# Choice of experts in finer steps, the first expert tile's rows from the ranks, half the context units later

## The chip, the cores and the metric

The kernel runs on one core of one Trainium2 chip. The metric is device time in microseconds. Each engine (PE for matmuls, DVE, ACT, POOL, and SP, which only issues transfers) runs its own instruction list; they meet at semaphores alone.

## The reference, cut to what matters

Two layers run in sequence, all in fp32, on 512 tokens of width 1024. The first ends in a hierarchical mixture of experts, 4 groups of 8 experts; the second begins with a projection of which the part called "context" here (a matmul of 256 context tokens, then a 5-tap convolution and a SiLU) needs nothing of the first layer.

```python
def hierarchical_moe(h, w_group, b_group, w_expert, b_expert, w_gate_up, w_down):
    g_logits = (t @ w_group + b_group).astype(jnp.float32)
    g_onehot = jax.nn.one_hot(jnp.argmax(g_logits, -1), N_GROUPS, dtype=jnp.float32)
    e_logits = (jnp.einsum('td,gde->tge', t, w_expert) + b_expert).astype(jnp.float32)
    e_sel = jnp.einsum('tge,tg->te', e_logits, g_onehot)
    top_vals, top_idx = lax.top_k(e_sel, TOP_K)      # 2 of the group's 8
    ...
    for g in range(N_GROUPS):
        gu = jnp.einsum('td,edf->tef', t, w_gate_up[g]).astype(jnp.float32)
        act = jax.nn.silu(a) * b * gate[:, g, :, None]
        y = y + jnp.einsum('tef,efd->td', act, w_down[g].astype(jnp.float32))
```

## The kernel before

**Up to the choice.** `out1_pe` ends the first mixer's output projection for four tiles of 128 tokens, transposes each normalised tile (`turn(t)`, `p.turns`, L154) and multiplies it with the router's 36 columns (`logits(t)`, L142). `route_dve` then chooses for all four tiles at once: the group by its largest logit, the best two of its experts by compares with rank numbers (`first_of`), and the sum AS of the two one-hot masks (signal `chosen`). `Chain` makes every step wait for the one before it on DVE.

**Ranks and indices.** `route_pe` counts with triangular and all-one matmuls how many earlier tokens want the same expert (`ranks`, L1192, L1194). `route_dve` makes from it prefix sums over the 32 experts (a copy and five shifted adds), where each token's row goes, and the mask S (`selected`); eight 128x32 matmuls (`row_ids`, L142) give the list of tokens of every expert tile (`token_ids`), and later `expert_ids`.

**Expert tiles.** There are eight groups g of four experts. Tile 2g ("home") holds 32 tokens for each; tile 2g+1 ("spill") holds overflow tokens of any expert. Here `up(j, third)` is 16 matmuls of 128x512 for one half of gate and up, `hidden(j)` two transposes, `down(j)` 16 matmuls. `experts_pool` fetches the tokens of tile j from memory (a gather, L1430); `rows(j)` on PE transposes them in eight matmuls (L154) into banks 0 and 1, and `rows(j)` on ACT and on DVE copy one bank each.

**Weights.** 96 pieces of 1 MB (twelve for each group: two times four for gate and up, four for down) go through SP's queue: the first 18 in the order `FIRST`, with the four context weights (`ctx_weights`, 1 MB each in rows of 1 KB) put in by `CTX_BEFORE`, and those in `AFTER_ROWS` held until `rows(0)` is done. `experts_sp` then issues pieces 18 to 95, each when the piece that held its buffer (15 in `SLOTS`, three used once in `ONCE`) is used up. ACT issues a spill tile's pieces conditionally (`spill`), by numbers that `spill_ids` loads into registers.

**Context.** `ctx_conv(p, a, b)` issues units a to b of 64. A unit is one matmul of 128x256 (two passes, two trace records). Eight units make a block b, in bank 2 or 7 in turn; `ctx_take(b)` on ACT empties the bank (`ctx_taken`), DVE makes the taps, `ctx_silu(b)` on ACT ends it. All 64 units stand between the logits and the first `up`, where PE otherwise waits. `keep_busy` is dummy work of five matmuls.

```python
        ctx_conv(p, 21, 46)
        p.wait_ge(S("selected"), 1)
        p.acc(bk(1, 32), sel, inc=S("row_ids"))
        ctx_conv(p, 46, 61)
```

Of the kernel before, what the change touches and what calls it, by code (L numbers as in the profile page):

```python
# [231 lines left out]
def program(nc, A, out):  # L232
# [973 lines left out]

    def route_dve(v):
        gl = lg[:, :, 0:4]
        el = lg[:, :, 4:36].rearrange("p t (g e) -> p t g e", g=4)
# [5 lines left out]
        c.red(gm[:, 0:4], gl, ALU.max)
        c.tt(v4(oh), gl, b4(gm[:, 0:4], 4), ALU.is_equal)
        c.tt(v4(ky), v4(oh), C["rank4"].unsqueeze(1).to_broadcast([P, 4, 4]), ALU.mult)
        c.red(km[:, 0:4], v4(ky), ALU.max)
        c.tt(v4(oh), v4(ky), b4(km[:, 0:4], 4), ALU.is_equal)
        es, e1, o1, o2, kk8, e2 = (rt0[:, 96 + 32 * j:128 + 32 * j] for j in range(6))  # L1220
        big = rt0[:, 320:448]
        bv = big.rearrange("p (t g e) -> p t g e", t=4, g=4)
        ohb = v4(oh).unsqueeze(3).to_broadcast([P, 4, 4, 8])
        c.tt(bv, el, ohb, ALU.mult)
        c.red(v8(es), big.rearrange("p (t g e) -> p t e g", t=4, g=4), ALU.add)
        m1, m2 = gm[:, 4:8], gm[:, 8:12]

        def first_of(dst, src, m):
            c.tt(v8(dst), v8(src), b4(m, 8), ALU.is_equal)
            c.tt(v8(kk8), v8(dst), C["rank8"].unsqueeze(1).to_broadcast([P, 4, 8]), ALU.mult)  # L1230
            c.red(km[:, 4:8], v8(kk8), ALU.max)
            c.tt(v8(dst), v8(kk8), b4(km[:, 4:8], 8), ALU.is_equal)

        c.red(m1, v8(es), ALU.max)
        first_of(o1, es, m1)
        c.stt(e2, o1, -3e38, es, ALU.mult, ALU.add)
        c.red(m2, v8(e2), ALU.max)
        first_of(o2, e2, m2)
        v.wait_ge(S("logit_m"), 4)
        v.up(v.e.memset(AS5[:, 128:160], 0.0), None)  # L1240
        c.tt(v4d(A1), ohb, v8(o1).unsqueeze(2).to_broadcast([P, 4, 4, 8]), ALU.mult)
        c.tt(v4d(A2), ohb, v8(o2).unsqueeze(2).to_broadcast([P, 4, 4, 8]), ALU.mult)
        c.tt(AS, A1, A2, ALU.add, inc=S("chosen"))


        pad = [MIX[:, 416 + 96 * j:512 + 96 * j].rearrange("p (s n) -> p s n", s=2) for j in range(2)]
# [2747 lines left out]
```

## Time and profile before

| | |
|---|---|
| runs of the kernel | 2337.04 us (median of 3), 2333.0 to 2340.38 |
| profiled execution: its own time (span, first to last instruction) | 2333.6 us |
| PE busy in it | 2212.6 us, 95% |
| DVE, ACT, POOL busy | 56%, 33%, 10% |
| memory read and written, mean over the span | 182 GB/s |

The span is the only time that the page gives for the profiled execution; no part of it outside the span is listed. PE is busy nearly always, but a share of the whole span says little of one stage: the page's DMA row in 40 slices reads 8 or 9 of ten from slice 4 to slice 10 (175 to 583 us), while PE's row reads 8 in slices 7 and 8 (350 to 467 us). Stages are therefore read one by one.

### The profile page before, as it was taken

How to read it: one execution, taken by the hardware profiler on the slowest of the kernel's cores; microseconds unless marked ns; L12 is line 12 of the kernel's file. 1: busy time of each engine (PE TensorE's matmuls, PEld its weight loads, DVE VectorE, ACT ScalarE, POOL GpSimd, SP SyncE). 2: the span in 40 equal slices, each digit the busy share in tenths (PEclk: the TensorE clock that was granted, in tenths of full speed). 3: DMA queues.
4: the chain of work that ended last, by engine and by line, in shares of the span. 5: the costliest groups of instructions: out<-in, count | busy, mean ns of one | idle time of the engine just before them, and what ended most of it. 6: DMA issues, size and time to landing. Idle time of an engine off the chain costs nothing.

```text
span 2333.6 us, 31012 instructions
## 1 busy us (share of the span) xinstructions
PE 2212.6 (95%) x12750; PEld 1721.4 (74%) x12750; DVE 1301.8 (56%) x2050; ACT 774.9 (33%) x1324; POOL 233.7 (10%) x219
## 2 busy tenths in 40 slices
PE   8999998899999999999999999999889889999997
PEld 6765843335889896788888888867777667788886
DVE  3355622215766786767686764436666645444444
ACT  3346111113534553512111120235556544222222
POOL 0000011101050440000000000002021040000000
PEclk9999999999999999999999999999999999999999
DMA  7548889998203114233343331111010203322321
GB/s 253 175 143 289 310 320 416 417 415 300 71 23 109 64 46 155 102 105 127 108 145 126 109 109 54 55 52 46 1 59 19 73 1 102 100 97 90 108 91 54
DMA packets 141084, 317.28 MB, mean 136 GB/s; under 512 B 16534, under 2 KB 77310, under 8 KB 128400
## 3 DMA queue, kind: packets, MB, share of 16 engines
q1 hardware_dynamic: 123136, 259.55, 31.1%
q0 software_dynamic: 16928, 52.55, 6.4%
q10 hardware_dynamic: 880, 3.20, 0.4%
q8 instruction: 101, 1.65, 0.3%
q14 instruction: 39, 0.32, 0.0%
HBM read 408.54 MB, written 15.79 MB: 182 GB/s over the span
## 4 chain that ended last, share of the span: by engine, by line
PE 79%; DVE 10%; DMA 5%; ACT 5%; issue 1%; POOL 0%; DVEq 0%; SPq 0%; ACTq 0%
PE PS L142 35%; PE PS L2995 12%; PE PS L721 5%; PE PS L1746 4%; PE PS L1453 4%; PE PS L154 3%; PE PS L2923 2%; PE PS L3623 2%; PE PS L1004 2%; PE PS L1465 2%; PE PS L148 2%; PE PS L3544 2%; DVE X L112 1%; DVE Rr L112 1%; PE PS L1056 1%
## 5 line engine op out<-in xcount | busy, mean ns | idle before, releaser
L142 PE MATMUL PS<-at,wH 128*128 128x512 f32 (+1 forms) x2144 | 564.0, 352 | 1.8 <-DVE at L112 1.8
L142 PEld LDWEIGHTS PS<-at,wH 128*128 128x128 f32 x2144 | 378.1, 189 | 61.1 <-issue 5.3
L142 PE MATMUL PS<-at,rest 128*128 128x512 f32 (+1 forms) x1072 | 376.4, 351 | 0.0
L2995 PE MATMUL PS<-wH,ac 128*128 128x512 f32 x880 | 278.1, 393 | 3.3 <-DVE hn L112 3.3
L142 PEld LDWEIGHTS PS<-at,rest 128*128 128x128 f32 x1072 | 202.6, 189 | 27.3
L112 DVE TENSOR_TENSOR rest<-ring,wH 128x2048 fp32r<-128x2048 f32 x66 | 150.3, 2289 | 95.5 <-ACT wH L135 95.4
L2995 PEld LDWEIGHTS PS<-wH,ac 128*128 128x128 f32 x880 | 165.2, 188 | 43.8 <-DVE hn L112 8.4
L135 ACT CAST wH<-ring 128x2048 fp32r<-128x2048 f32 x66 | 124.6, 1906 | 201.0 <-PE PS L2995 201.0
L2995 PE MATMUL PS<-rest,ac 128*128 128x512 f32 x440 | 171.4, 390 | 0.0
L112 DVE TENSOR_TENSOR hn<-PS,gate 128x512 f32<-128x512 f32 x120 | 83.0, 692 | 86.0 <-PE PS L2995 79.3
L135 ACT CAST ac<-sil 128x1536 fp32r<-128x1536 f32 (+1 forms) x22 | 27.8, 1264 | 296.0 <-DVE sil L112 296.0
L112 DVE TENSOR_TENSOR sil<-sil,PS 128x512 f32<-128x512 f32 x66 | 39.1, 598 | 153.6 <-PE PS L142 153.6
L2995 PEld LDWEIGHTS PS<-rest,ac 128*128 128x128 f32 x440 | 82.7, 188 | 17.0 <-issue 0.7
L132 ACT ACTIVATE sil<-PS 128x512 f32<-128x512 f32 x66 | 34.7, 527 | 178.2 <-PE PS L142 178.2
L1453 PE MATMUL PS<-ring,AT 128*32 128x512 f32 x288 | 87.5, 600 | 4.8 <-DMA R<-in_w_gate_up_dram 3.0
L112 DVE TENSOR_TENSOR H<-H,hn 128x512 f32<-128x512 f32 x120 | 83.0, 692 | 4.1
L135 ACT COPY R<-PS 128x512 f32<-128x512 f32 (+4 forms) x105 | 47.4, 471 | 107.9 <-PE PS L142 58.6
L142 PE MATMUL PS<-Rr 96*128 96x512 f32 (+3 forms) x384 | 80.8, 345 | 1.3 <-ACT Rr L135 1.3
L123 DVE TENSOR_REDUCE sm<-PS 128x1 f32<-128x768 f32 x64 | 60.9, 952 | 36.7 <-PE PS L142 36.2
L1453 PE MATMUL PS<-R,AT 128*32 128x512 f32 x400 | 75.2, 616 | 5.5 <-DMA HIw<-in_w_gate_up_dram 2.4
L154 PE MATMUL PS<-con,R 128*128 128x128 f32 (+1 forms) x452 | 66.3, 278 | 14.3 <-DVE R L116 8.0
L154 PEld LDWEIGHTS PS<-con,R 128*128 128x128 f32 (+1 forms) x452 | 50.8, 140 | 37.0 <-DVE R L116 11.6
(503 smaller groups left out, 4503.4 us busy)
## 6 DMA issues: line engine op xcount, KB each, us to landing
R<-in_w_gate_up_dram SPq DMA_DIRECT2D x25, 1024.0 KB, 13.9
R<-in_w_gate_up_dram ACTq DMA_DIRECT2D x25, 1024.0 KB
HIw<-in_w_ada_dram POOLq DMA_DIRECT2D x24, 1024.0 KB, 5.6
ring<-in_w_ffn_gate_dram SPq DMA_DIRECT2D x22, 1024.0 KB, 5.4
ring<-in_w_ffn_up_dram SPq DMA_DIRECT2D x22, 1024.0 KB, 5.4
ring<-in_w_ffn_down_dram SPq DMA_DIRECT2D x22, 1024.0 KB, 4.9
ring<-in_w_gate_up_dram SPq DMA_DIRECT2D x18, 1024.0 KB, 11.8
ring<-in_w_gate_up_dram ACTq DMA_DIRECT2D x18, 1024.0 KB
```

The lines of the kernel that those rows point to most:

```text
L112: return self.up(self.e.tensor_tensor(dst, a, b, op), inc)
L123: return self.up(self.e.tensor_reduce(dst, a, AX, op, negate=neg), inc)
L135: return self.up(self.e.copy(dst, src), inc)
L142: ins = self.e.matmul(out, l, r, start=k == 0, stop=k == len(pairs) - 1)
L148: ins = self.e.matmul(o, l, r, start=True, stop=True)
L154: ins = self.e.transpose(o, i_, ident[0:i_.shape[0], 0:i_.shape[0]])
L721: ins = p.e.matmul(bk(t), x, w[:, k, :], start=r == 0 and k == 0 and i == 0, stop=r == 1 and k == 3 and i == 2)
L1004: ins = p.e.matmul(bk(g % 3), x, w, start=k == 0 and i == 0, stop=k == 7 and i == 2)
L1453: ins = p.e.matmul(PS[32 * c:32 * c + 32, 512 * b:512 * b + 512], hgT[j % 2][:, 4 * third + k, 32 * c:32 * c + 32], expert_slot(g, third, ...
L1465: ins = p.e.matmul(PS[32 * c:32 * c + 32, 512 * (5 + h):512 * (6 + h)], abT[j % 2][:, 128 * f + 32 * c:128 * f + 32 * c + 32], expert_slot ...
L1746: ins = p.e.matmul(bk(i % 4), x, y[:, k, :], start=b == 0 and k == 0 and n == 0, stop=b == 1 and k == 3 and n == 2)
L2995: ins = p.e.matmul(bk(4 + n_dn % 3), a_, b_, start=start and i == 0, stop=stop and i == len(terms) - 1)
```

## The change

The logits of a tile start when half of it is copied. The choice becomes `choose(v, t0, n)`, run for tiles 0 and 1, for tile 2 and for tile 3 apart, with DVE's max and max_index of eight; the rank matmuls of tiles 0 to 2 precede the last choice. A compare S0 (128x512) and four matmuls of one column give the tokens of tile 0 (`first_ids`), for which the first gather now waits in place of `token_ids`. Prefix sums become two scans. `rows(0)` goes to banks 5 and 6, both copied by ACT, and `row_ids` stands inside `up(0, 0)`. Six context units move behind `up(0, 1)`, 32 into groups 2 and 3; context weights 2 and 3 are loaded behind piece 26 into buffers that pieces 9 and 10 have left, and pieces 14 and 15 no longer wait for `rows(0)`. Blocks 4 to 7 of the context all use bank 7.

```diff
@@ out1_pe, route_pe @@
+            for k in range(8):
+                if k % 4 == 0:
+                    p.wait_ge(S("h1_T_copy"), 2 * t + k // 4 + 1)
...
         logits(2)
-        ctx_conv(p, 2, 6)
         turn(3)
-        ctx_conv(p, 6, 8)
+        ctx_conv(p, 2, 3)
         logits(3)
-        ctx_conv(p, 8, 21)
+        ctx_conv(p, 3, 5)
...
-    CTX_W = [(R[:, 4096:6144], ("o", 4)), (H[:, 4096:6144], ("gate_kept", 64)), (R[:, 8192:10240], ("normed_T", 4)), (R[:, 0:2048], ("out1", 8))]
-    ctx_bank = lambda b: (2, 7)[b % 2]
+    CTX_W = [(R[:, 4096:6144], ("o", 4)), (H[:, 4096:6144], ("gate_kept", 64)), (H[:, 0:2048], ("down", 4)), (H[:, 2048:4096], ("down", 4))]
+    ctx_bank = lambda b: 2 if b in (0, 2) else 7
...
-                p.wait_ge(S("ctx_taken"), b - 1)
+                p.wait_ge(S("ctx_taken"), b - 1 if b < 4 else b)
...
+        p.e.matmul(at(3, 5), ones, tile(2, 2), start=False, stop=False)
+        ctx_conv(p, 5, 7)
+        p.wait_ge(S("chosen"), 3)
+        p.e.matmul(at(3, 4), C["U"], tile(3, 1), start=False, stop=False)
+        ins = p.e.matmul(at(4, 5), ones, tile(3, 1), start=False, stop=True)
         p.up(ins, S("ranks"))
-        ctx_conv(p, 21, 46)
-        p.wait_ge(S("selected"), 1)
-        p.acc(bk(1, 32), sel, inc=S("row_ids"))
-        ctx_conv(p, 46, 61)
+        ctx_conv(p, 7, 9)
+        p.wait_ge(S("first_rows"), 1)
+        p.acc(bk(3, 1), [(S0[:, 128 * t:128 * t + 128], less[:, t:t + 1]) for t in range(4)], inc=S("first_row_m"))
+        ctx_conv(p, 9, 24)
@@ choose (tiles t0 to t0 + n), route_dve @@
+        c.red(gm[:, ts_], gl, ALU.max)
+        c.tt(of4(oh), gl, of(gm, 4), ALU.is_equal)
+        c.tt(of4(ky), of4(oh), C["rank4"].unsqueeze(1).to_broadcast([P, n, 4]), ALU.mult)
+        c.red(km[:, ts_], of4(ky), ALU.max)
+        c.tt(of4(oh), of4(ky), of(km, 4), ALU.is_equal)
+        c.ts(of4(pen), of4(oh), 1.0, 3e38, ALU.subtract, ALU.mult)
+        c.tt(bv, el, of4(pen).unsqueeze(3).to_broadcast([P, n, 4, 8]), ALU.add)
...
+            v.up(v.e.max(mx8[:, 8 * t:8 * t + 8], big[:, 32 * t:32 * t + 32]), None)
...
+            v.up(v.e.max_index(ix8[:, 8 * t:8 * t + 8].bitcast(U32), mx8[:, 8 * t:8 * t + 8], big[:, 32 * t:32 * t + 32]), None)
+        c.copy(ixf[:, 8 * t0:8 * t0 + 8 * n], ix8[:, 8 * t0:8 * t0 + 8 * n].bitcast(U32))
...
+        for A_, j in ((A1, 0), (A2, 1)):
+            v.tt(v32(A_)[:, ts_, :], iot[:, 0:32].unsqueeze(1).to_broadcast([P, n, 32]),
...
+        c.tt(S0.rearrange("p (t n) -> p t n", t=16), bc(m0, 32), iot[:, 1:33].unsqueeze(1).to_broadcast([P, 16, 32]), ALU.is_equal, inc=S("first_rows"))
...
-        for j, sh in enumerate((1, 2, 4, 8, 16)):
-            src, dst = pad[j % 2], pad[1 - j % 2]
-            c.tt(dst[:, :, 16:48], src[:, :, 16:48], src[:, :, 16 - sh:48 - sh], ALU.add)
+        for j, x in enumerate((spill, free)):
+            v.up(v.e.tensor_tensor_scan(tally[:, j, 1:33], ones[:, 0:32], x, 0.0, ALU.mult, ALU.add), None)
+        v.wait_ge(S("first_row_m"), 1)
+        v.ts(tidx0, bk(3, 1), 4096.0, None, ALU.add, inc=S("first_ids"))
@@ weights, gathers @@
-    FIRST = [5, 1, 3, 4, 12, 13, 0, 2, 7, 8, 16, 6, 17, 9, 10, 11, 14, 15]
-    CTX_BEFORE = {5: 0, 12: 1, 0: 2, 7: 3}
-    AFTER_ROWS = (11, 14, 15)
+    FIRST = [5, 1, 14, 3, 4, 12, 13, 0, 2, 15, 7, 8, 16, 6, 17, 9, 10, 11]
+    CTX_BEFORE = {5: 0, 12: 1}
+    AFTER_ROWS = (11,)
...
             expert_piece(s, m)
+            if m == 26:
+                for i in (2, 3):
+                    ctx_weights(s, i)
...
-        g.wait_ge(S("token_ids"), 1)
+        g.wait_ge(S("first_ids"), 1)
...
+            if j == 1:
+                g.wait_ge(S("token_ids"), 1)
@@ experts_pe, experts_act @@
+                if j == 0 and third == 0 and k == 2:
+                    p.wait_ge(S("selected"), 1)
+                    p.acc(bk(1, 32), sel, inc=S("row_ids"))
...
         rows(0)
-        ctx_conv(p, 61, 64)
+        ctx_conv(p, 24, 26)
...
             up(2 * g, 1)
+            if g == 0:
+                ctx_conv(p, 26, 32)
+                rows(1)
...
             down(2 * g)
+            if g in (2, 3):
+                ctx_conv(p, 16 * g, 16 * g + 8)
             if g not in (0, NG - 1):
                 up(2 * g + 1, 1)
             if g + 1 < NG:
                 rows(2 * g + 3)
+            if g in (2, 3):
+                ctx_conv(p, 16 * g + 8, 16 * g + 16)
...
                 rows(2 * g + 3)
                 ids = spill_ids(g + 1)
             if 1 <= g < 5:
+                if g in (2, 3):
+                    ctx_take(a, 2 * g)
+                    ctx_take(a, 2 * g + 1)
```

**PE from the last choice to the first expert tile.** In the rows, `L1056` (now `L1059`) is a context unit, `L154` (`L155`) the transposes of `rows(0)`, `L1453` (`L1486`) an `up`; `s_exp1` is `ctx_taken`. Before:

```order
L142 MATMUL PS<-X,MIX 128x32 [waits s_chosen]
L142 MATMUL PS<-X,MIX 128x32 x7
L1056 MATMUL PS<-AT,R 128x256 x2
L1056 MATMUL PS<-AT,R 128x256 [waits s_exp1,s_x_in3]
L1056 MATMUL PS<-AT,R 128x256 x7
L1056 MATMUL PS<-AT,R 128x256 [waits s_exp1]
L1056 MATMUL PS<-AT,R 128x256 x4
L154 MATMUL PS<-con,MIX 128x128 [waits s_rows0]
L154 MATMUL PS<-con,MIX 128x128 x7
L1056 MATMUL PS<-AT,R 128x256 x3
L1453 MATMUL PS<-ring,AT 32x512 [waits s_rowsD,s_w_home00,s_rowsA,s_exp1]
```

`row_ids` leads this stretch, and 15 units follow it up to `rows(0)`. Now, from the last rank matmul:

```order
L1205 MATMUL PS<-MIX,con 128x32
L1059 MATMUL PS<-AT,R 128x256 x2
L143 MATMUL PS<-MIX 128x1 [waits s_first_rows]
L143 MATMUL PS<-MIX 128x1 x3
L1059 MATMUL PS<-AT,R 128x256 x7
L1059 MATMUL PS<-AT,H 128x256 [waits s_exp1,s_ada_w1]
L1059 MATMUL PS<-AT,H 128x256 x7
L155 MATMUL PS<-con,MIX 128x128 [waits s_rows0]
L155 MATMUL PS<-con,MIX 128x128 x7
L1059 MATMUL PS<-AT,H 128x256 [waits s_exp1]
L1059 MATMUL PS<-AT,H 128x256
L1486 MATMUL PS<-ring,AT 32x512 [waits s_w_home00,s_rowsA]
```

The eight 128x32 matmuls have left the place ahead of `rows(0)`, four of one column have come, and 15 context units stand behind these, where 15 stood behind `row_ids` before and 25 ahead of it.

**PE at the end of group 2.** `L154` (`L155`) with the wait for `s_rows1` is `rows(7)`, `L690` (`L691`) is `keep_busy`, and `s_w_home01` is the next home tile's weights. Before:

```order
L1453 MATMUL PS<-R,AT 32x512 x3
L154 MATMUL PS<-con,MIX 128x128 [waits s_rowsD,s_rowsA,s_rows1]
L154 MATMUL PS<-con,MIX 128x128 x7
L690 MATMUL PS<-con 128x128 x5
L1453 MATMUL PS<-HIw,AT 32x512 [waits s_w_home01]
L1453 MATMUL PS<-HIw,AT 32x512
```

Nothing but dummies stands between the transposes and the next `up`. Now:

```order
L1486 MATMUL PS<-R,AT 32x512 x3
L155 MATMUL PS<-con,MIX 128x128 [waits s_rowsD,s_rowsA,s_rows1]
L155 MATMUL PS<-con,MIX 128x128 x7
L1059 MATMUL PS<-AT,H 128x256 [waits s_exp1]
L1059 MATMUL PS<-AT,H 128x256 x7
L691 MATMUL PS<-con 128x128 x5
L1486 MATMUL PS<-HIw,AT 32x512 [waits s_w_home01]
L1486 MATMUL PS<-HIw,AT 32x512
```

A block of eight units with a wait for `ctx_taken` stands between `rows(7)` and the next home tile; another block (not shown) stands ahead of the spill tile's second half.

**ACT at the end of group 2.** `TENSOR_LOAD sm` rows are the register loads of `spill_ids(3)`, `s_masked` stands for DVE's taps. Before:

```order
L1529 TENSOR_LOAD sm
L1529 ISA x2
L1530 TENSOR_LOAD sm
L1530 ISA x2
L132 ACTIVATE AT<-MIX,cwc 128x256 [waits s_masked] x2
L1536 ISA [waits s_up]
L1536 DMA HIw<-in_w_gate_up_dram 128x2048
```

ACT goes from the loads straight to the SiLUs of the context. Now, with `s_o` for `ctx_conv`:

```order
L1568 TENSOR_LOAD sm
L1568 ISA x2
L1569 TENSOR_LOAD sm
L1569 ISA x2
L136 COPY AT<-PS 128x256 [waits s_o] x2
L133 ACTIVATE AT<-MIX,cwc 128x256 [waits s_masked] x2
L1575 ISA [waits s_up]
L1575 DMA HIw<-in_w_gate_up_dram 128x2048
```

The two copies that empty bank 7 stand behind the eight register loads, and behind the copy of `rows(7)` ahead of those.

## Rows read from the trace of the kernel before

**Rows 1.** Table by stage: stretch, us; PE, PEld, DVE, ACT, POOL busy; PEclk, DMA share, GB/s.

```profile
246.00:250.00 4.00, 4.00 (x19) 3.25 (x19) 3.72 (x7) 0.20 (x1) 0.00 (x0) 1.00 1.09 390
282.00:286.00 4.00, 4.00 (x24) 3.64 (x24) 3.01 (x18) 0.37 (x1) 0.00 (x0) 1.00 1.02 426
294.00:316.00 22.00, 22.00 (x163) 13.01 (x163) 6.16 (x19) 5.87 (x11) 5.10 (x5) 1.00 0.60 218
370.00:530.00 160.00, 138.44 (x1170) 58.96 (x1166) 36.27 (x70) 20.23 (x37) 17.10 (x17) 0.97 1.01 416
429.00:433.00 4.00, 3.91 (x24) 0.98 (x28) 0.00 (x0) 0.00 (x0) 0.00 (x0) 0.57 1.01 416
```

**Rows 2.** PE's timeline around the choice and the first expert tiles.

```profile
274.05 1.98 PE L142 MATMUL PS<-X,MIX 128*128 128x36 f32 x16
...
293.64 1.87 PE L142 MATMUL PS<-X,MIX 128*128 128x32 f32 x16
295.35 6.72 PE L1056 MATMUL PS<-AT,R 128*128 128x256 f32 x30
301.90 1.05 PE L154 MATMUL PS<-con,MIX 128*128 128x128 f32 x8
...
304.18 0.62 PE L1453 MATMUL PS<-ring,AT 128*32 128x512 f32 x1
...
312.30 0.59 PE L1453 MATMUL PS<-ring,AT 128*32 128x512 f32 x1
```

**Rows 3.** DVE's timeline, same stretch: last normalised tile, choice, ranks, indices.

```profile
268.95 1.28 DVE L120 SCALAR_TENSOR_TENSOR H<-H,X 128x1024 f32<-128x1024 f32 x1
...
270.69 0.20 DVE L112 TENSOR_TENSOR X<-PS,X 128x36 f32<-128x36 f32 x1 [0.34 <-PE PS L142]
276.07 0.20 DVE L112 TENSOR_TENSOR X<-PS,X 128x36 f32<-128x36 f32 x1 [5.18 <-PE PS L142]
...
281.23 0.29 DVE L112 TENSOR_TENSOR MIX<-MIX 128x128 f32<-128x128 f32 x1
...
282.96 0.19 DVE L117 TENSOR_SCALAR MIX<-PS 128x32 f32<-128x32 f32 x1 [0.54 <-PE PS L1194]
...
291.61 1.22 DVE L112 TENSOR_TENSOR MIX<-con,MIX 128x1024 f32<-128x1024 f32 x1
...
295.55 0.19 DVE L116 TENSOR_SCALAR sm<-PS 128x32 uint32<-128x32 f32 x1 [0.93 <-PE PS L142]
```

**Rows 4.** POOL's timeline: the first gather's issue.

```profile
296.63 1.09 POOL L1430 DMA_INDIRECT MIX<-h1d,sm  x1 [17.58 <-DVE sm L116]
```

**Rows 5.** The gathers' line (L1430) over the kernel: issue to landing.

```profile
DMA to landing us min/median/max: 4.5/8.3/12.7
```

**Rows 6.** The h1d write of L1167, issued at 270.5 under the weight stream: landing.

```profile
DMA to landing us min/median/max: 9.5/9.5/9.5
```

**Rows 7.** ACT's timeline at the end of group 2.

```profile
381.22 0.59 ACT L135 COPY AT<-PS 128x512 f32<-128x512 f32 x1 [0.23 <-PE PS L154]
386.06 0.51 ACT L132 ACTIVATE AT<-MIX,cwc 128x256 f32<-128x256 f32 x1 [4.25 <-issue]
```

**Rows 8.** What PE waited for between 380 and 410.

```profile
PE PS L1453 <- DMA ring<-in_w_gate_up_dram: 2.7, 1, 2.7
PE PS L1453 <- DMA X<-in_w_gate_up_dram: 0.9, 1, 0.9
PE PS L1465 <- DMA R<-in_w_down_dram: 0.7, 1, 0.7
```

**Rows 9.** Three expert pieces (L1405) issued at 316 into idle queues: landing.

```profile
DMA to landing us min/median/max: 5.3/6.4/7.5
```

**Rows 10.** The chain that ended last: one expert piece in the full stream.

```profile
391.95 14.01 DMA R<-in_w_down_dram
```

**Rows 11.** PE's timeline in group 4: the first matmul behind a gap.

```profile
429.09 1.06 PE L1453 MATMUL PS<-HIw,AT 128*32 128x512 f32 x1 [2.41 <-DMA gate<-in_w_gate_up_dram]
```

More of the change, by code:

```diff
@@ L988, in logits @@
             p.wait_ge(S("conv_w"), 1)
-            p.acc(bk(3 + t % 2, 36), [(hT[:, k, 128 * t:128 * t + 128], wr[:, k, :]) for k in range(8)], inc=S("logit_m"))
+            for k in range(8):
+                if k % 4 == 0:
+                    p.wait_ge(S("h1_T_copy"), 2 * t + k // 4 + 1)
+                ins = p.e.matmul(bk(3 + t % 2, 36), hT[:, k, 128 * t:128 * t + 128], wr[:, k, :], start=k == 0, stop=k == 7)
+            p.up(ins, S("logit_m"))
         def ctx_turn(t):
@@ L1188, in route_pe @@
     def route_pe(p):
-        p.wait_ge(S("chosen"), 1)
-        tile = lambda q, n: v32(AS)[:, q, :].unsqueeze(1).to_broadcast([P, n, 32])
+        tile = lambda q, n: AS_of(q).unsqueeze(1).to_broadcast([P, n, 32])
+        at = lambda a_, b_: bk(0, 160).rearrange("p (t n) -> p t n", t=5)[:, a_:b_, :]
+        p.wait_ge(S("chosen"), 2)
         p.e.matmul(bk(0, 160), C["U"], AS5, start=True, stop=False)
-        for q in range(4):
-            ins = p.e.matmul(bk(0, 160).rearrange("p (t n) -> p t n", t=5)[:, q + 1:5, :], ones, tile(q, 4 - q),
-                             start=False, stop=q == 3)
+        p.e.matmul(at(1, 5), ones, tile(0, 4), start=False, stop=False)
@@ L1196, in route_pe @@
+        p.e.matmul(at(2, 5), ones, tile(1, 3), start=False, stop=False)
+        p.e.matmul(at(3, 5), ones, tile(2, 2), start=False, stop=False)
[3 more added lines that the diff above has]
+        ins = p.e.matmul(at(4, 5), ones, tile(3, 1), start=False, stop=True)
         p.up(ins, S("ranks"))
-        ctx_conv(p, 21, 46)
-        p.wait_ge(S("selected"), 1)
-        p.acc(bk(1, 32), sel, inc=S("row_ids"))
@@ L1200, in route_pe @@
-        ctx_conv(p, 46, 61)
+        ctx_conv(p, 7, 9)
+        p.wait_ge(S("first_rows"), 1)
+        p.acc(bk(3, 1), [(S0[:, 128 * t:128 * t + 128], less[:, t:t + 1]) for t in range(4)], inc=S("first_row_m"))
+        ctx_conv(p, 9, 24)
     def route_act(a):
+        for b in range(3):
+            ctx_take(a, b)
+        for h in range(2):
+            a.wait_ge(S("rows_T"), h + 1)
+            a.cast(hgT[0][:, 4 * h:4 * h + 4, :], bk(5 + h).rearrange("p (k t) -> p k t", k=4), inc=S("rowsA"))
@@ L1214, in route_dve @@
         c = Chain(v)
[L1215 to L1246, printed above, removed]
@@ L1249, in route_dve @@
         small = [MIX[:, 800 + 8 * j:808 + 8 * j] for j in range(12)]
-        less = MIX[:, 1984:2000]
-        for x in pad:
-            v.up(v.e.memset(x[:, :, 0:16], 0.0), None)
-        for j in range(4):
-            c.ts(less[:, 4 * j:4 * j + 4], C["tid"], 4096.0 - (S_ if j == 3 else 0.0), None, ALU.subtract)
+        v.wait_ge(S("ranks"), 1)
+        r4, m4 = bk(0, 128).rearrange("p (t n) -> p t n", t=4), m0.rearrange("p (t n) -> p t n", t=4)
+        v.settle()
+        v.tt(m4[:, 0:3, :], r4[:, 0:3, 0:4], v32(AS)[:, 0:3, 0:4], ALU.mult)
+        v.tt(m4[:, 3, :], r4[:, 3, 0:4], AS3[:, 0:4], ALU.mult)
+        c.tt(S0.rearrange("p (t n) -> p t n", t=16), bc(m0, 32), iot[:, 1:33].unsqueeze(1).to_broadcast([P, 16, 32]), ALU.is_equal, inc=S("first_rows"))
         magic = 12582912.0
-        spill, free = pad[0][:, 0, 16:48], pad[0][:, 1, 16:48]
-        v.wait_ge(S("ranks"), 1)
-        c.ts(spill, bk(0, 32, 128), 48.5, 1.0 / 32, ALU.subtract, ALU.mult)
+        spill, free = wants[:, 0:32], wants[:, 32:64]
+        v.ts(spill, bk(0, 32, 128), 48.5, 1.0 / 32, ALU.subtract, ALU.mult)
         v.ts(free, bk(0, 32, 128), 32.5, None, ALU.is_lt)
@@ L1264, in route_dve @@
         c.ts(spill, spill, magic, 0.0, ALU.subtract, ALU.max)
[L1265 to L1269 removed]
+        v.settle()
+        for j, x in enumerate((spill, free)):
+            v.up(v.e.tensor_tensor_scan(tally[:, j, 1:33], ones[:, 0:32], x, 0.0, ALU.mult, ALU.add), None)
+        incl, before, taken = tally[:, 0, 1:33], tally[:, 0, 0:32], tally[:, 1, 1:33]
+        v.wait_ge(S("first_row_m"), 1)
+        v.ts(tidx0, bk(3, 1), 4096.0, None, ALU.add, inc=S("first_ids"))
         c.stt(RV, before, 64.0, C["hh"], ALU.mult, ALU.add)
[L1273 removed]
+        v.tt(freecode, free, taken, ALU.mult)
         c.ts(RV, RV, 512.0, -1.0, ALU.mult, ALU.add)
@@ L1518, in silu @@
             a.wait_ge(S("hidden"), j - 1)
-            a.fn(sil[j % 2], bk(2 + j % 2, 256), ACT.Silu, inc=S("silu"))
+            a.fn(sil[j % 2], bk(hid_bank(j), 256), ACT.Silu, inc=S("silu"))
         def y(j):
@@ L1542, in experts_act @@
         a.fn(sm[:, 64:65], ones[:, 0:1], ACT.Silu)
-        rows(0)
-        ctx_take(a, 7)
         ids = spill_ids(0)
+        spill(0, 0)
         rows(1)
+        ctx_take(a, 3)
         for g in range(NG):
-            spill(g, 0)
+            if g:
+                spill(g, 0)
             if g:
@@ L1607, in ctx_taps @@
                 c.stt(to, src, cwc[:, b, tap:tap + 1], to, ALU.mult, ALU.add, inc=S("ctx_sum") if tap == 4 else None)
-        rows(0)
         rows(1)
```

84 lines of the change are left out of this document (55 added, 29 removed).

## The prediction

> **What bounds the kernel now.** I read first the table by stage, to see whether transfers or PE fill each stretch. From 370 to 530 the DMA share is 1.01 at 416 GB/s and PE is busy for 138.44 of 160 us: the experts' weights set the pace there, and PE waits. From 294 to 316 it is the reverse: PE is busy for all 22.00 us, with a DMA share of 0.60 [rows 1], so transfers stand idle for 0.40 x 22 = 8.8 us. The stream of pieces 18 to 95 starts when the first home tile is used up, so the whole stage moves with the start of the first spill tile, 312.30 [rows 2]; but no earlier start can give more than those 8.8 us. Second I read the timelines of PE, DVE and POOL for the chain that leads there: last logits read by DVE at 276.07, last mask 281.23, ranks 282.96, token list 295.55 [rows 3], gather issued 296.63 [rows 4], rows transposed 301.90, first `up` 304.18 [rows 2]. PE has no gap in it: the context units are what it does while DVE chooses.
>
> **The chain up to the first expert tile.** *Logits.* The last tile is normalised at 268.95 + 1.28 = 270.2 [rows 3]. Its logits ran from 274.05 to 276.03, behind six context units; one is left. A unit is 6.72 / 15 = 0.45 us [rows 2], so five give 2.2: logits end at 273.8. *Choice.* It took from 276.07 to 281.23 + 0.29 = 281.52, in steps of about 0.2 [rows 3]. The pass for tile 2, some 15 steps from 270.69 + 0.20, ends at about 274.2, just behind those logits; that for tile 3 has 13 steps, 2.6 us, behind one read of 0.2, so it ends at 277.1, 4.4 earlier. max and max_index don't occur in the trace; I count them as the other small steps, 0.2; at 0.5 each it is 1 us more, at nothing 1 us less. *Ranks.* 281.52 to 282.96 was 1.4 for five matmul groups; two are left behind the last mask: 0.7, so 277.8. *First rows.* Two small steps and a 128x512 compare, for which I take 0.7, between 0.29 for 128 and 1.22 for 1024 columns [rows 3]: 278.9. Four matmuls and one step are half of the eight and their step (293.64 [rows 2] to 295.74 [rows 3], 2.1) with a little for the hand-over: 280.2. From token list to gather it was 0.9 [rows 3, 4], so the gather is issued at 281.1, 15.5 earlier. The scans are beside this path.
>
> *Landing.* This is the term without a row of its own. Before, the gather met idle transfers; at 281 the share is 1.02 [rows 1]. Gathers took 4.5 to 12.7, median 8.3 [rows 5], and a write issued from the same queue at 270.5 in this very stretch took 9.5 [rows 6]. I take 9.0, nearest to that write: 290.1. The ends are 4.5 and 12.7. The Trainium skill, "DMA: Bandwidth & Descriptors", section "Issuing engines are not separate DMA queues", says that transfers of all issuing engines share the same 16 DMA engines and interleave, which speaks against an early gather under another queue's stream; the 9.5 against 4.5 agrees. If it did not hold, the sum would come out by 3.6 us lower.
>
> *PE.* Behind the ranks stand 17 units and four small matmuls, 7.7 + 0.9, so PE is free at 286.5 and idle for 3.6. Transposes to first `up` took 304.18 - 301.90 = 2.3 [rows 2]; with one unit less on the path I take 2.0: 292.1, or 12.1 earlier.
>
> **What is given back at once.** From first `up` to the spill tile it was 312.30 - 304.18 = 8.1 [rows 2]. `row_ids` comes into it (1.87, of which 1.7 between its neighbours [rows 2]), six units (2.7), and about 0.8 because the second gather now waits for a token list made inside this stretch and ACT loads registers ahead of the second tile's copy: 13.3 and 305.4. The stream's start moves by s = -6.9. With a landing of 4.5 PE itself is the limit at 286.5, so s = -10.5; with 12.7, s = -3.2. As 6.9 is less than 8.8, the transfers' idle time can take it. Pieces 14 and 15 cost nothing: the same 18 pieces are through before the stream starts, in idle time if need be.
>
> **The full stream.** Context weights 2 and 3 lay ahead of it and now lie in it. A piece of 1 MB is 1.05 / 0.416 = 2.5 us [rows 1]. These come in rows of 1 KB: from 246 to 250, where such rows flow among others, 390 GB/s need a share of 1.09, against 426 at 1.02, or 1.17 times the time for a byte [rows 1]; if half the bytes there were context weights, 1.34. I take 3.1 each, so +6.2 (bounds 5.0 and 6.7). Of s, -0.7 is left.
>
> **PE in groups 2 and 3.** Sixteen units a group are 16 x 0.45 = 7.2. The second block stalls besides: bank 7 is emptied by ACT behind the copy at 381.22 and the register loads, during which ACT does nothing until 386.06, 4.25 us of it without a releaser [rows 7]. So PE waits about 386.06 - 381.22 = 4.8 each time, and is 2 x (7.2 + 4.8) = 24.0 later. Three waits for weights in these groups vanish: 2.7 + 0.9 + 0.7 = 4.3 [rows 8]. PE then falls behind its weights by 24.0 - 4.3 - 6.2 = 13.5. How much of that the transfers bear is the depth of the queue: a piece in the full stream lands 14.0 after its issue [rows 10], one in an idle queue after 5.3 [rows 9], so 8.7 us of work lie queued. The remaining 13.5 - 8.7 = 4.8 is idle time of a resource that is busy to the end of the stage, and is not got back: +4.8. The waits behind it (21.6 us without PE work from 370 to 530 [rows 1], the 4.3 among them) let PE catch up, no more.
>
> **The clock.** A gap of 2.41 us ahead of 429.09 was followed by matmuls of 1.06 us [rows 11] where full speed has 0.59 [rows 2]; the granted clock was 0.57 from 429 to 433 [rows 1], the lower level (1.2 GHz) for most of it. Four steps at twice their time, some 3.4 us, cost half of that, 1.7. The two stalls are longer than that gap. From 370 to 530 its mean is 0.97 beside those 21.6 us of gaps [rows 1], so it follows not every gap, and I take one of two: +1.7.
>
> **Sum.** -6.9 + 6.2 + 4.8 + 1.7 = +5.8. The profiled execution's span of 2333.6 would become 2339.4; it is 3.4 below the median of the runs, 2337.0, and to that I add: **2342.8 us**. 0.3%, or 7.0 us, is about what a measurement of this kernel can tell from no change.
>
> **Rivals.** *Clock and late gather (slower).* The clock falls in both stalls (+1.7), and also in the idle 3.6 ahead of the first tile (+1.7): 2346.2; if the gather lands after 12.7 as well, 3.7 more, 2349.9. This is slower than can be missed as soon as any 1.2 us come on top of the forecast. The gaps are longer than that of rows 11; against it, one clock loss early may fall into the 1.9 us of idle transfers that s leaves. The Trainium skill, "TensorE: Matmul & The Clock Gate", section "Why this matters for your kernels", warns that idle gaps between bursts of matmuls send the array back to the lower clock; rows 11 agree, and by it this rival would be the forecast. *Transfers alone.* If PE's lag stays within the depth, because the queue bears more than 8.7 or more of the idle 21.6 comes early, only s and the weights count: -0.7, 2336.3, and with s = -10.5 it is 2332.7. For it: share 1.01; against it: 24 us of work in two groups that had 4.3 of waits. *All kept (faster).* If the context weights slip in for nothing and PE's work fits its waits, s alone remains: 2330.1, and 2328.2 where the gather lands early and s takes all of the 8.8. Rows 1 with a share of 1.01 speak against it. *No earlier tile.* If another queue entry holds the gather up until the stream thins out, near 294, s is about -3.2 and the time 3.7 over the forecast, 2346.5; its chance is counted with the first rival, whose late gather it is.
>
> **Chances.** Forecast 0.40 (0.07 of it above 7.0 more than before), clock or late gather 0.28, transfers alone 0.20 (0.01 of it below -7.0), all kept 0.12 (0.09 below). So faster 0.10, same 0.55, slower 0.35. The range runs from 2331, just under the transfers' rival with the early landing, to 2352: s = -3.2, both clock losses and the upper price of the weights give 2337.0 - 3.2 + 6.7 + 4.8 + 3.4 + 1.7 = 2350.4, and a stall a little longer makes the rest. About 0.1 lies below and 0.1 above.
>
> **What would show it.** Steps right: last mask near 277, gather 0 issued near 281 and landed near 290, first `up` near 292, spill tile near 305; in groups 2 and 3 PE waits of some 5 us for ACT's copy of bank 7, and a stretch between 385 and 440 where the DMA share is below 1. Wrong: a share of 1.01 throughout (transfers alone), a gather that lands within 5 us, PE waits for `ctx_taken` below 2 us, or PEclk of 1.00 behind both stalls.

## The result and the profile after

The changed kernel takes 2348.45 us (median of 6 runs, 2347.18 to 2351.48), the kernel before 2335.28 (6 runs, 2332.67 to 2340.96): a ratio of 1.0051, interval 1.0039 to 1.0063, or 12 us slower. The profiled execution has a span of 2346.5, the one of before 2333.6: +12.9. From the page of the changed kernel, the span and PE's total:

```profile
span 2346.5 us, 31053 instructions
...
PE 2216.0 (94%) x12760; PEld 1722.3 (73%) x12760; DVE 1304.1 (56%) x2072; ACT 774.8 (33%) x1325; POOL 233.9 (10%) x219
```

PE's busy time has hardly changed (2212.6 us before). The table by stage (columns as in rows 1) tells where the time went:

```profile
370.00:530.00 160.00, 143.17 (x1146) 69.41 (x1139) 34.72 (x68) 19.65 (x39) 16.15 (x16) 0.97 0.92 373
390.00:400.00 10.00, 9.27 (x54) 6.39 (x58) 1.89 (x4) 1.55 (x4) 0.00 (x0) 0.83 0.98 406
400.00:410.00 10.00, 9.48 (x84) 3.51 (x80) 1.12 (x2) 0.59 (x1) 1.00 (x1) 1.00 0.42 153
430.00:440.00 10.00, 7.64 (x26) 6.34 (x26) 3.55 (x8) 1.23 (x4) 0.00 (x0) 0.66 0.99 414
440.00:450.00 10.00, 9.48 (x82) 3.56 (x85) 1.12 (x2) 0.90 (x2) 0.10 (x1) 1.00 0.15 34
```

From 370 to 530 the DMA share is 0.92 where it was 1.01 [rows 1]. The missing share lies in two holes: 0.42 from 400 to 410 and 0.15 from 440 to 450, that is (1.01 - 0.42) x 10 + (1.01 - 0.15) x 10 = 14.5 us of idle transfers. Ahead of each, PE ran at a granted clock of 0.83 and 0.66.

**The head came out as worked out, up to the gather.** The second tile's logits, in the trace of before and then in that of the changed kernel, where the timeline goes on to the first spill tile:

```profile
265.17 1.87 PE L142 MATMUL PS<-X,MIX 128*128 128x36 f32 x16
```

```profile
266.07 1.87 PE L992 MATMUL PS<-X,MIX 128*128 128x36 f32 x16
...
290.69 1.16 PE L155 MATMUL PS<-con,MIX 128*128 128x128 f32 x8 [3.02 <-DMA MIX<-h1d,sm]
...
293.48 1.06 PE L1486 MATMUL PS<-ring,AT 128*32 128x512 f32 x1
...
295.18 0.59 PE L1486 MATMUL PS<-ring,AT 128*32 128x512 f32 x1
...
296.14 1.97 PE L143 MATMUL PS<-X,MIX 128*128 128x32 f32 x16
...
306.02 1.04 PE L155 MATMUL PS<-con,MIX 128*128 128x128 f32 x8
308.42 0.62 PE L1486 MATMUL PS<-ring,AT 128*32 128x512 f32 x1 [1.36 <-ACT AT L136]
```

This execution ran 0.9 late there, as it did at the first tile's logits (257.96 against 257.06), ahead of all that was changed; so I count from the second tile's. The first `up` comes at 293.48 - 266.07 = 27.4 (before 39.0), the first spill tile at 42.35 (before 47.1 [rows 2]): 4.8 earlier, 3.9 on the span's own scale. Of 11.6 us at the first `up` more than half is gone fifteen microseconds later. On DVE's timeline, one slow step of the last choice, the last mask, and the 128x512 compare:

```profile
275.87 0.91 DVE L118 TENSOR_SCALAR X<-X 128x4 f32<-128x4 f32 x1
...
278.10 0.19 DVE L113 TENSOR_TENSOR MIX<-MIX 128x32 f32<-128x32 f32 x1
...
279.29 0.69 DVE L113 TENSOR_TENSOR MIX<-X,con 128x512 f32<-128x512 f32 x1
```

The gather in the chain that ended last:

```profile
282.17 8.47 DMA MIX<-h1d,sm
```

**The stall.** ACT's timeline and PE's at the end of groups 2 and 3:

```profile
385.73 0.59 ACT L136 COPY AT<-PS 128x512 f32<-128x512 f32 x1 [0.23 <-PE PS L155]
390.31 0.37 ACT L136 COPY AT<-PS 128x256 f32<-128x256 f32 x1 [3.99 <-issue]
```

```profile
377.76 3.72 PE L1059 MATMUL PS<-AT,H 128*128 128x256 f32 x16
...
390.73 5.39 PE L1059 MATMUL PS<-AT,H 128*128 128x256 f32 x16 [4.59 <-ACT AT L136]
...
419.66 3.72 PE L1059 MATMUL PS<-AT,H 128*128 128x256 f32 x16
...
432.36 6.75 PE L1059 MATMUL PS<-AT,H 128*128 128x256 f32 x16 [4.32 <-ACT AT L136]
```

The copy of the rows at 385.73, then the register loads, then at 390.31 the copy that frees bank 7; PE's second block waits 4.59 and 4.32 for it, and takes 5.39 and 6.75 us where the first blocks take 3.72. Between them PE waits for nothing else of note from 380 to 440:

```profile
PE PS L1059 <- ACT AT L136: 8.9, 2, 4.6
```

No wait for weights is left there. The kernel before has 8.5 us of them in the same stretch: the 4.3 of rows 8, which end at 410, and from 410 to 440

```profile
PE PS L1453 <- DMA gate<-in_w_gate_up_dram: 2.4, 1, 2.4
PE PS L1453 <- DMA HIw<-in_w_gate_up_dram: 1.8, 1, 1.8
```

On SP's timeline one sees the other end. The row at 385.48 is of four pieces, issued within 20.30 us where the same four took 11.31 before: the last of them had to wait for its buffer. The next hole ends with the piece at 448.44, which went at 425.43 before. Before, then now:

```profile
380.97 11.31 SPq L1405 DMA_DIRECT2D R<-in_w_down_dram  x4
...
425.43 0.33 SPq L1405 DMA_DIRECT2D R<-in_w_down_dram  x1
```

```profile
385.48 20.30 SPq L1426 DMA_DIRECT2D R<-in_w_down_dram  x4
...
448.44 0.33 SPq L1426 DMA_DIRECT2D R<-in_w_down_dram  x1
```

The first matmul behind the experts, before and now:

```profile
553.17 0.50 PE L1746 MATMUL PS<-Xr,Hr 128*128 128x512 f32 x1
```

```profile
566.47 0.50 PE L1788 MATMUL PS<-Xr,Hr 128*128 128x512 f32 x1
```

It starts 300.40 us after the second tile's logits, 288.00 before: +12.4, in this execution the whole of the loss.

### The profile page after: what moved, and what is told of

The parts are those of the page before. It is cut to its first block, busy times and chain, and to the rows that moved or that the text cites. A ratio compares the mean times of both kernels' runs of the same rounds, so it can differ in the third digit from the quotient of the medians.

```text
span 2346.5 us, 31053 instructions
## 1 busy us (share of the span) xinstructions
PE 2216.0 (94%) x12760; PEld 1722.3 (73%) x12760; DVE 1304.1 (56%) x2072; ACT 774.8 (33%) x1325; POOL 233.9 (10%) x219
## 4 chain that ended last, share of the span: by engine, by line
PE 77%; DVE 11%; ACT 5%; DMA 4%; issue 1%; ACTq 0%; POOL 0%; DVEq 0%; SPq 0%; POOLq 0%
PE PS L143 34%; PE PS L3038 12%; PE PS L722 5%; PE PS L1486 4%; PE PS L155 3%; PE PS L1788 3%; PE PS L2966 2%; PE PS L1498 2%; PE PS L3666 2%; PE PS L1008 2%; DMA R<-in_w_gate_up_dram 2%; DVE X L113 2%; PE PS L3587 2%; PE PS L149 1%; DVE Rr L113 1%
## 5 line engine op out<-in xcount | busy, mean ns | idle before, releaser
L113 DVE TENSOR_TENSOR sil<-sil,PS 128x512 f32<-128x512 f32 x66 | 39.1, 598 | 153.7 <-PE PS L143 153.7
L1486 PE MATMUL PS<-ring,AT 128*32 128x512 f32 x288 | 88.6, 604 | 7.3 <-DMA R<-in_w_gate_up_dram 5.9
L155 PE MATMUL PS<-con,R 128*128 128x128 f32 (+1 forms) x452 | 66.6, 278 | 14.9 <-DVE R L117 8.1
L155 PEld LDWEIGHTS PS<-con,R 128*128 128x128 f32 (+1 forms) x452 | 50.8, 139 | 38.1 <-DVE R L117 11.7
L143 PEld LDWEIGHTS PS<-Rr 96*128 96x128 f32 (+1 forms) x384 | 64.7, 188 | 16.5 <-issue 3.5
```

Source lines behind the costliest of these rows:

```text
L113: return self.up(self.e.tensor_tensor(dst, a, b, op), inc)
L143: ins = self.e.matmul(out, l, r, start=k == 0, stop=k == len(pairs) - 1)
L155: ins = self.e.transpose(o, i_, ident[0:i_.shape[0], 0:i_.shape[0]])
L1486: ins = p.e.matmul(PS[32 * c:32 * c + 32, 512 * b:512 * b + 512], hgT[j % 2][:, 4 * third + k, 32 * c:32 * c + 32], expert_slot(g, third, ...
```

## The experiments

All ratios are to the kernel before. "Spill" and "end" are taken from PE's timeline of each profiled execution, counted from the second tile's logits: to the first spill tile's first matmul, and to the first matmul behind the experts. Each value is of one execution. The eight with the changed kernel's head (all but the kernel before, choice alone, move alone and the two with a new head) have spill tiles from 40.5 to 43.6, and the changed kernel's own two executions lie 1.7 apart there and 3.8 at the end. A difference of that size in these columns shows nothing by itself.

| run | ratio (interval) | spill | end |
|---|---|---|---|
| kernel before | 1 | 47.1 | 288.0 |
| changed kernel | 1.0051 (1.0039 to 1.0063) | 42.4 | 300.4 |
| the same, in a later job | 1.0051 (1.0038 to 1.0064) | 40.7 | 296.6 |
| bank 7 emptied first | 1.0001 (0.9987 to 1.0015) | 41.8 | 287.3 |
| the same, late units left out | 1.0003 (0.9990 to 1.0017) | 41.9 | 284.7 |
| the same, late weights left out | 0.9985 (0.9973 to 0.9997) | 43.6 | 285.3 |
| dummies in the stalls | 1.0061 (1.0040 to 1.0082) | 40.5 | 293.6 |
| dummies, in the later job | 1.0035 (1.0022 to 1.0048) | 40.7 | 294.4 |
| choice alone | 1.0038 (1.0020 to 1.0056) | 53.8 | 295.2 |
| move alone | 1.0049 (1.0031 to 1.0067) | 49.9 | 295.1 |
| late blocks spread | 0.9997 (0.9986 to 1.0008) | 40.5 | 283.1 |
| spread, new head | 0.9989 (0.9975 to 1.0003) | 39.1 | 284.2 |
| spread, new head, wide rows | 0.9988 (0.9979 to 0.9996) | 39.3 | 283.8 |

**Bank 7 emptied first.**

```diff
             y(2 * g)
             spill(g, 2)
+            if g in (2, 3):
+                ctx_take(a, 2 * g)
             if g not in (0, NG - 1):
...
                 if g in (2, 3):
-                    ctx_take(a, 2 * g)
                     ctx_take(a, 2 * g + 1)
```

> ACT empties bank 7 of the first late block right behind the spill issue of group 2 (and 3), ahead of the SiLU, the copy of the rows and the register loads; nothing else changes. Theory (the stalls for bank 7 and the half clock behind them cost the time): PE's waits of 4.6 and 4.3 us go, the second blocks take 3.65 us in place of 5.4 and 6.75, PE's lag at the end of group 3 falls from about 23 to about 10 us, DMA idle in 400 to 450 falls from 14.4 us to about 3 us, and the time to about 2336 (2334 to 2339). Rival (32 more units in a stage that transfers bound cost their own time, stall or not): 14.4 us of units remain as lag, transfers still idle, time 2342 to 2346.

Measured 2337.13, within the theory's bounds: the place of one copy is worth some 12 us. PE's two second blocks and the stage:

```profile
383.66 3.62 PE L1059 MATMUL PS<-AT,H 128*128 128x256 f32 x16
...
419.04 3.62 PE L1059 MATMUL PS<-AT,H 128*128 128x256 f32 x16
```

```profile
370.00:530.00 160.00, 148.81 (x1240) 69.84 (x1242) 36.16 (x70) 21.48 (x41) 17.10 (x17) 1.00 1.00 407
```

No block waits, all four take 3.6 to 3.7 us, the clock is 1.00 and the share 1.00.

**Dummies in the stalls.** `keep_busy(p, 2, 20)` ahead of the second blocks.

> Twenty dummy matmuls of 128x128 (about 4.5 us) stand ahead of the second late block in groups 2 and 3, where PE waits for bank 7: the stall keeps its length, but PE is busy in it. Theory: the granted clock stays at full speed, the blocks take 3.65 us, and 1.7 + 3.1 = 4.8 us of lag go, so the time falls by about 4 to 5 us, to 2344. Rival (the lower clock cost nothing, since PE waits behind it anyway): unchanged, 2348 (2347 to 2350).

The granted clock behind the two stalls did what was expected:

```profile
389.00:393.00 4.00, 3.85 (x20) 3.29 (x19) 1.45 (x3) 0.25 (x1) 0.00 (x0) 1.00 1.02 417
429.00:433.00 4.00, 4.00 (x22) 3.56 (x22) 1.70 (x4) 0.20 (x1) 0.00 (x0) 1.00 1.01 422
```

The time didn't show it: 2348.1, with an interval of 0.4%. So it was run again, beside the changed kernel.

> The kernel with dummies in the two stalls once more, in five rounds, beside the changed kernel itself: its four runs before lay at 2345 twice and at 2351 twice, and told nothing. Theory (half clock behind the stalls costs some 5 us of lag): 4 to 6 us below the changed kernel. Rival (lag that is spared there is given back behind the experts): within 2 us of the changed kernel.

> The changed kernel as it is, for comparison in the same job: 2347 to 2350 in either theory.

Now 2345.19 against 2350.75 (a little above the 2347 to 2350 expected), ratios 1.0035 and 1.0051. The intervals of the four runs overlap; some 3 to 4 us for the clock is likely, less than the 4.9 us by which the two blocks were long (5.39 + 6.75 - 2 x 3.6), and in time it is not settled. In the stage it is seen. The first execution with dummies:

```profile
370.00:530.00 160.00, 148.87 (x1237) 74.94 (x1236) 34.84 (x69) 20.08 (x39) 16.13 (x16) 1.00 0.95 386
```

The share is 0.95 in both executions with dummies and 0.92 in both of the changed kernel: 0.03 x 160 = 4.8 us less of idle transfers with the clock kept, and some 10 us still idle for the stall and the units. That the stall is the larger part shows in time too: with the clock kept, 8 us of loss remain in the better of the two jobs.

**Late units left out.** In `ctx_conv`, on top of the run that empties bank 7 first.

```diff
+            if b >= 4 and 0 < k < 7:
+                continue
```

> As the run that empties bank 7 first, and of each of the four late blocks only the first and the last matmul are kept, so that 24 of the 32 late units are left out (their part of the context is not computed). Theory (without the stall the remaining 14.4 us of units fit into PE's waits and the queue's depth): at most 3 us faster than that run, about 2334. Rival (the units themselves cost): faster than that run by 6 to 11 us.

2337.9: in this execution the experts end 2.6 earlier, and the time is no shorter. Three quarters of the units, 24 x 0.45 = 10.8 us of PE's work, cost next to nothing once the stall is gone. The stage, and the longest of the waits for weights that come back from 380 to 450:

```profile
370.00:530.00 160.00, 142.73 (x1198) 61.60 (x1194) 36.27 (x70) 21.51 (x41) 17.14 (x17) 0.98 1.01 414
```

```profile
PE PS L1488 <- DMA gate<-in_w_gate_up_dram: 2.2, 1, 2.2
```

**Late weights left out.** The two loads behind piece 26 are taken out of that same run, with the waits for them.

> As the run that empties bank 7 first, but context weights 2 and 3 are not loaded (their units read what the buffers hold, so that part of the context is not what it should be). Theory (the two loads of 1 MB in rows of 1 KB cost 6 us of a stage that transfers bound): the pieces behind piece 26 land 6 us earlier, the last expert tile ends 4 to 6 us earlier than in that run, time about 2332. Rival (PE, with 32 units more, is the limit there, and the loads are hidden): within 1.5 us of that run.

2332.93 against 2337.13, ratios 0.9985 and 1.0001: about 4 us, the theory's sign and two thirds of its size. The two intervals overlap, so the time alone does not show it. The landings do: the piece behind piece 26 landed 4.7 us after it, 9.2 in the run that empties bank 7 first, so it came 4.6 earlier, where 6 were expected. The experts' end came 2.1 earlier, not 4 to 6, behind a spill tile that was 1.8 later in this execution. The loads are not free, but the stream had some room for them. Their price is most of the 5 us by which the spill tile comes earlier, which may be why the run that empties bank 7 first is no faster than the kernel before.

**Choice alone.** `CTX_W`, banks, `FIRST`, `AFTER_ROWS` and `SLOTS` as before; the rest of the change stays.

```diff
-        ctx_conv(p, 9, 24)
+        ctx_conv(p, 9, 61)
...
         rows(0)
-        ctx_conv(p, 24, 26)
+        ctx_conv(p, 61, 64)
```

> The new choice, ranks, scans and first gather, but all 64 context units ahead of the first expert tile, and the context weights, their banks and pieces 14 and 15 as in the kernel before. Theory (ahead of the first tile PE is the limit, so that a shorter choice alone brings nothing): PE busy without a gap, first up at 303 to 304, first spill tile at 313 to 315, time 0 to 3 us above the kernel before, about 2337. Rival (the choice's chain was the limit): first up 4 to 12 us earlier than 304.2, time 2325 to 2331.

2343.26, slower than either theory said. The first part held: first `up` at 304.53, as before, behind PE's own work. What neither had is behind it:

```profile
304.53 0.62 PE L1483 MATMUL PS<-ring,AT 128*32 128x512 f32 x1
...
306.39 1.97 PE L143 MATMUL PS<-X,MIX 128*128 128x32 f32 x16
...
314.45 1.16 PE L155 MATMUL PS<-con,MIX 128*128 128x128 f32 x8 [0.80 <-DMA MIX<-h1d,sm]
318.67 0.62 PE L1483 MATMUL PS<-ring,AT 128*32 128x512 f32 x1 [3.06 <-ACT AT L136]
```

`row_ids` now stands inside the first `up`, so the second gather's list comes late (0.80 of wait at 314.45), and ACT's copy of those rows, behind its register loads, later still (3.06). The first spill tile starts 6.7 us later than before.

**Move alone.** The old choice with the late blocks, weights and piece order, bank 7 emptied first.

> The old choice, ranks and first gather, with the context units, the context weights, the order of the pieces and the emptying of bank 7 as in the run that empties it first; 32 units stay ahead of the first up, three of them behind rows(0). Theory (the choice is on the path only once the units are moved): PE idles some 10 us ahead of rows(0), first up at 303 to 304, first spill tile 0 to 1 us earlier than before, so 46 to 47 from the second tile's logits in place of 41.9, and the time 3 to 5 us above the run with both, about 2341. Rival (the choice brings nothing in any order): time equal to that run's, 2337.

2346.96: the sign is right, the size over twice what was expected, and the spill tile comes at 49.9 instead of 46 to 47. PE waits for the masks, the selection and the gather, with nothing to fill in, and in the stage from 294 the granted clock is 0.72:

```profile
281.53 0.54 PE L1192 MATMUL PS<-MIX,con 128*128 128x160 f32 x2 [2.87 <-DVE MIX L112]
...
293.93 3.62 PE L142 MATMUL PS<-X,MIX 128*128 128x32 f32 x16 [4.11 <-DVE X L112]
...
303.16 1.97 PE L154 MATMUL PS<-con,MIX 128*128 128x128 f32 x8 [2.90 <-DMA MIX<-h1d,sm]
...
306.94 0.62 PE L1456 MATMUL PS<-ring,AT 128*32 128x512 f32 x1
```

```profile
294.00:316.00 22.00, 19.11 (x120) 11.66 (x124) 6.39 (x19) 4.10 (x9) 5.11 (x5) 0.72 0.39 121
```

The expectation had left out that clock. So choice and move cost 9 and 11 us alone, and nothing together once bank 7 is emptied first: the shorter choice brings PE nothing while the units fill its time, and the move lays the old chain bare. What the choice alone lost lies between the first `up` and the spill tile, where `row_ids` now stands; no run moved `row_ids` alone there.

**Late blocks spread.** One block behind the home tile's `down` in each of groups 2 to 5.

```diff
-            if g in (2, 3):
-                ctx_conv(p, 16 * g, 16 * g + 8)
+            if 2 <= g < 6:
+                ctx_conv(p, 8 * g + 16, 8 * g + 24)
...
-            if g in (2, 3):
-                ctx_take(a, 2 * g)
+            if 2 <= g < 6:
+                ctx_take(a, g + 2)
```

> As the run that empties bank 7 first, but one late block of eight units in each of groups 2, 3, 4 and 5 behind its home tile's down, where two stood in each of groups 2 and 3; the SiLUs and taps of blocks 4 to 7 move back to match. Theory (units are free as long as they stay below PE's waits for weights, some 5 us a group, and the queue's depth): DMA share 1.01 throughout 370 to 530, PE no wait for bank 7, time equal to that run's within 2 us, 2335 to 2338. Rival (each block costs its 3.65 us wherever it stands): 2342 to 2346.

2335.55, as the theory said, with a share of 1.01 for the stage:

```profile
370.00:530.00 160.00, 147.78 (x1223) 68.14 (x1225) 35.23 (x69) 20.98 (x40) 16.92 (x17) 1.00 1.01 411
```

**New head.** On top of that:

```diff
+        keep_busy(p, 4, 13)
         rows(0)
+        p.wait_ge(S("selected"), 1)
+        p.acc(bk(1, 32), sel, inc=S("row_ids"))
...
-                ctx_conv(p, 26, 32)
                 rows(1)
+                ctx_conv(p, 26, 32)
```

> As the spread run, and ahead of the first spill tile: row_ids behind the transposes of rows(0) and no longer inside the first up, rows(1) ahead of the six units behind the first home tile, and 13 dummies where PE waits for the first gather. Theory (there ACT's chain from the token list over the register loads to the copy of rows(1), and PE's half clock behind the idle 3 us, set the first spill tile): the list of tokens comes 4 us earlier, PE runs at full speed, the first spill tile 2.5 to 3.5 us earlier than in the changed kernel, counted from the second tile's logits (42.35 there), so 39 to 40, and the time 2 to 3 us below the spread run. Rival (the transfers take the earlier start up, as they take half of the context weights' cost): no difference in time.

The first spill tile came at 39.1 as expected, without the wait for ACT:

```profile
307.04 0.62 PE L1484 MATMUL PS<-ring,AT 128*32 128x512 f32 x1
```

That is 1.4 earlier than in the spread run, less than two executions of the changed kernel differ by. The time did not follow: 2335.88 against 2335.55, and the experts' end came 1.1 later. This is the rival's outcome, but its way is not shown: PE's waits for weights from 310 to 380 were 4.0 us in all here, 4.8 in the spread run.

**Wide rows.** Context weights 2 and 3 as halves of one matrix, 2 KB a row.

> As the run with the new head, and the two late context weights loaded as halves of one matrix in rows of 2 KB in place of 1 KB. Theory (their price in the stream is set by the short rows, and half of it is room anyway): the two land within 5.0 to 5.5 us in place of 6.0 and the time is 0 to 1.5 us lower, 2334 to 2336, 1 to 3 us below the kernel before. Rival (a piece is a piece): landing as now, time as now.

2335.04, ratio 0.9988: the only complete version whose whole interval lies below 1, by 3 us, though barely. From the landing of piece 26 to that of the piece behind the two weights it was 7.9 us, 9.1 in the run with the new head: the transfers got 1.2 us shorter, as the theory had it. In time no difference from that run (0.9989) shows.

## Why the prediction was right or wrong

The measured 2348.45 lies inside the range (2331 to 2352), but 5.7 above the forecast of 2342.8, and slower by more than 0.3%, which had 0.35. It is the first rival's ground, and its mechanism in part: the clock fell as it said, the gather was not late. Against its own base the forecast is further off: it added 5.8 to 2337.0, and beside the result the kernel before took 2335.28, so that 12 to 13 came where 5.8 was forecast.

**Right.** The chain to the gather: last mask expected at 277.1, seen at 278.29 (0.9 of it the late execution); the compare took 0.69 of an expected 0.7; gather issued at 282.17 (281.1), landed 8.47 later (9.0). That it came so near was partly luck, as the landing had been a choice between 4.5 and 12.7. By the Trainium skill ("DMA: Bandwidth & Descriptors", "Issuing engines are not separate DMA queues") the transfers of all issuing engines share the same DMA engines; 8.47 under the stream, where 4.5 was the least [rows 5], agrees. PE's waits for bank 7, expected at 4.8, were 4.59 and 4.32. The two late context weights cost 6.0 against 6.2. That the lag turns into idle transfers is what the holes show.

**The stream's start, s.** The step "13.3 and 305.4" was short: from first `up` to spill tile it took 14.94. Two of its first steps ran at half clock (1.06 instead of 0.59), 0.8 us together, and PE waited 1.36 for ACT's copy, behind register loads that a list made inside the first `up` had delayed; I had 0.8 for the second and nothing for the first. With the slightly later start, s was -4.8, or -3.9 on the span, in place of -6.9. By the new head's run such microseconds are worth little.

**The lag.** The step that failed is "24.0 - 4.3 - 6.2 = 13.5", with the idle time of 4.8 from it; measured were 14.5. Three things were wrong. I took off the 6.2 of the context weights as if PE's lag began behind them; but by group 2 PE had already waited for the stream that they delay. The second half of its home tile, `up(4, 1)`, before and now:

```profile
364.02 0.62 PE L1453 MATMUL PS<-ring,AT 128*32 128x512 f32 x1
```

```profile
362.92 0.62 PE L1486 MATMUL PS<-ring,AT 128*32 128x512 f32 x1 [2.69 <-DMA R<-in_w_gate_up_dram]
```

So the whole lag counted against the queue's depth. Second, the half clock went into the sum as 1.7, when it lengthens the lag inside the stage: the two blocks were 4.9 us long, and the tile that begins at 362.92 ran slower too, by 1.8. In the chain that ended last, that tile and one like it at full speed:

```profile
362.92 8.77 PE PS L1486 x64
...
406.71 7.00 PE PS L1486 x64
```

Third, the 4.3 of vanished waits was read from a window that ends at 410. Up to the piece issued at 425.43 the kernel before has one more, the 1.8 for `HIw`: 6.0 in all. Counted so, 24.0 - 0.7 (shorter stalls) + 4.9 + 1.8 - 6.0 = 24.0. The traces agree: the piece that ends the second hole was issued 23.0 later than before, by a PE that had come to the tile above 1.1 earlier, so the lag is 24.1. Against a depth of 8.7 it gives 15.3 to 15.4 us of idle transfers, near the 14.5 seen; the depth itself was measured by no run. The rule of the Trainium skill ("TensorE: Matmul & The Clock Gate", "Why this matters for your kernels") that gaps send the array to the lower clock agrees with the 0.83 and 0.66 behind the stalls and the 1.00 with dummies in them.

**The sum by its measured terms.** -3.9 (start) + 6.0 (context weights: the piece ahead of them landed 3.7 earlier than before, at 341.33, the piece behind them 2.3 later, at 350.42) + 14.5 (idle transfers) = +16.6, of which the spans show +12.9. The rest, 3.7, is not shown term by term. Part of it is room in the stream, as the run without those weights found 4.6 of the 6.0 in its landings and about 4 in time. Against the sum of the prediction these are +3.0 for the start, -0.2 for the weights, +9.7 for the idle transfers, -1.7 for the clock, now in the lag, and -3.7. That the time still lies inside the range is luck: without those 3.7, which no term foresaw, it would be at the upper edge.

**Rivals.** "Transfers alone" (2336.3) was the picture without the stall: that run gave 2337.13. "All kept" is ruled out by the new head: a spill tile 8.0 earlier than before brought 2.6, and by the interval at most 5.8. "No earlier tile" fell: the gather landed as expected.

## What to carry to other kernels

When a step with a single buffer is put into a stage that another engine paces, look at what stands ahead of the instruction that empties the buffer, on its own engine: here eight register loads that no wait names, and moving one copy ahead of them was worth some 12 us. Filler work is free only up to the lag that the paced queue can bear, so add up lag, stalls and the clock behind them, and compare that with the depth once, without taking off delays that the waiting engine has already sat through. Where filler covers a serial chain, do not judge moving the filler or shortening the chain alone: here they cost 11 and 9 us apart and came out even together.

## What was not expected of the hardware

The same gap does not cost the same each time. The changed kernel's second profiled execution has the two stalls as well:

```profile
389.40 6.13 PE L1059 MATMUL PS<-AT,H 128*128 128x256 f32 x16 [4.59 <-ACT AT L136]
...
431.75 5.41 PE L1059 MATMUL PS<-AT,H 128*128 128x256 f32 x16 [4.29 <-ACT AT L136]
```

Waits of 4.59 and 4.29 us, as good as the 4.59 and 4.32 of the first, are followed by blocks of 6.13 and 5.41, where the first had 5.39 and 6.75.

This execution was 3.8 us ahead at the experts' end (296.6 against 300.4) and 0.2 at the end of the span's matmuls. A lead of 3 us in one stage was thus lost behind it. Where it went is not shown; it may be why several runs above differ at the experts' end and not in time.

A step of one DVE instruction on a 128x4 tile took 0.91 at 275.87, where its neighbours take 0.16; POOL cleared a buffer from 274.92 on at that moment. No run here tells whether that is the cause.
